# Weight chunks fetched behind 36 modulation pieces, and the first three output tiles multiplied feature by feature

## The chip, the cores and the metric

The kernel runs on one core of a Trainium2 chip. The core has TensorE (PE, matrix products into PSUM), VectorE (DVE), ScalarE (ACT), GpSimd (POOL, unused here) and SyncE (SP), which issues every transfer. All times are device microseconds (us) of the whole kernel; lower is better. Three runs of the kernel before gave 2514.09, 2517.24 and 2517.44 us.

## What is computed

Two transformer blocks on 256 tokens of width 1024, all in f32. Only the very start matters here: the condition vector gives shift, scale and gate by a large matrix-vector product, the input is normed and modulated, and the first SwiGLU follows.

```python
cond = silu(c)
mod = cond @ w_ada + b_ada                     # 1024 x 9216
sh1, sc1, gt1, ... = split(mod, 9)
u = rmsnorm(x, g1) * (1 + sc1) + sh1
a, b = split(u @ w_ffn1_in, 2)                 # 1024 x 5632
h = x + 0.5 * gt1 * ((silu(a) * b) @ w_ffn1_out)
...                                            # token mixing, FFN 2, block 2
```

## The kernel before

**Data.** X holds the tokens transposed, as 8 features groups ("features", k = 0 to 7) of 128 channels by 256 tokens. Every matrix is cut into chunks of 128 x 1024 numbers (512 KB); one chunk of a first FFN matrix makes one output tile of 128 channels, 8 products over k. Products are made in three matmuls each, since both factors are split into a rounded part ("high") and a remainder ("low"): high by high, high by low, low by high (L1404 to L1406). So one output tile is 24 matmuls of 256 columns.

**A weight chunk's way.** SyncE fetches it into one of four raw buffers (`fetch`, L1372). ScalarE rounds it into its own slot (`high`, L1652, own<-raw). VectorE subtracts that from the raw chunk (`low`, L1976), which frees the raw buffer; so fetch n waits for low n - 4. A slot is free when TensorE has done with the chunk that was in it (four slots at this stage).

**Modulation.** The nine sections of `w_ada` are 16 pieces of 128 x 512 each (256 KB, `modload`, L1362, into SCR or MODS). One pass of VectorE (`mod`, L1992) multiplies a piece by the condition vector and adds up; each pass is followed by a short accumulator read. The first 16 pieces give the scale sc1 (coefficient `CF`, L2013), the next 16 the shift sh1; both are needed before the first feature. 20 pieces can be on chip at the start; from piece 36 on, a piece's load waits for the pass of the piece four before it.

**The norm.** ScalarE squares the eight features (L1671), TensorE sums them over channels with a matrix of ones (L1431), ScalarE takes the root (`stat`, L1684) and VectorE the reciprocal (`root`, L2038). A feature is then a product on VectorE (`rms`, NT, L2112), a rounding on ScalarE (Uh, L1717) and a remainder on VectorE (Ul, L2119).

**Order.** Nothing is scheduled at run time. `schedule` calls methods of a `Plan`, each `put` appends one piece of work to a list, and every engine walks the list and takes what is its own, in that order. `chunk` is called when TensorE comes to a new chunk n: it puts the highs up to chunk n + 3 (`split_next`), then modulation passes by `rate` (`background`), and whatever was postponed. `low_parts` puts the lows of the highs so far, each followed by the next fetch; it does nothing for chunks above `low_limit`. `norm_tiles` puts the features; where it is given `tiles`, and nothing fills the time, it takes three chunks and puts `products` of all three after each feature. That way is in use later in the kernel, in the stages with other names than w1. In the first stage (`p.rms("n1", ...)`) the features are put alone, and the tiles come one after the other: chunk 0 is the "gate" half of output tile 0 (evicted by ScalarE with Silu, L1786, SA), chunk 1 its "up" half (multiplied in by VectorE, L2142, GT), then chunks 2 and 3 for tile 1. The product is split again (Hh on ScalarE, L1793, Hl on VectorE, L2148).

Of the kernel before, what the change touches and what calls it, by code (L numbers as in the profile page):

```python
# [25 lines left out]
SLABS = [[0, 1]] + [list(range(i, i + FS)) for i in range(2, FT, FS)]  # L26
# [4 lines left out]
LAT, CTX, BOTH = (0, S), (S, 2 * S), (0, 2 * S)  # L31
# [18 lines left out]
RING = 4  # L50
LEAD = 3
# [664 lines left out]
def schedule(total):  # L716
    p = Plan(total)
# [2 lines left out]
    while p.mod_fetch(0) and p.mod_loads < 16:  # L720
        pass
    p.put("xload")
    for _ in range(RING):
        p.fetch()
    p.put("cond", q=0, n=0)

    t = p.tally(LAT, False, lambda k: None)
    for k in range(KT):
        p.square(t, k, 0)
    p.rms("n1", 0, 0, "g1", (0, 0), None, ahead=LEAD)  # L730
    for who in (1, 2):
        p.put("condload", q=who, n=who)
        p.put("cond", q=who, n=who)
# [6 lines left out]
            p.put("rawshift", k=k, q=0, f=3)  # L740
        p.rate = 0.0

    main = p.ffn("w1", "w1o", LAT, [(("w1", 0), "half", 0, 2)], False, then={len(SLABS) - 1: before_raw}, raw="nm")
    p.put("ctxload")
    for _ in range(12):
        next(main)
    p.rate = 1.7
    p.put("maskload")
    for i in range(14):
        p.later(5 + i, lambda i=i: p.put("rotary", k=i))  # L750
# [22 lines left out]
    t = p.tallies.pop(LAT)  # L773
    raw = [p.raw_tile("wpqk", 0, 0, 6)]
# [15 lines left out]
    made, raw = raw, [None] * RAW  # L790
# [42 lines left out]
    n1 = 8  # L833
# [12 lines left out]
    for pair in range(4):  # L846
# [3 lines left out]
        c = p.chunk("wbr", pair)  # L850
# [24 lines left out]
    t = p.tallied(LAT, 1e-6, (0, 1))  # L875
# [156 lines left out]
    first = p.group("aqk", LAT, (*key_ctx["qs"], query))  # L1032
# [56 lines left out]
    t = p.tallies.pop(LAT)  # L1089
# [23 lines left out]
    t = p.tallied(LAT, 1e-5, (0, 0))  # L1113
# [1401 lines left out]
```

## Time and profile before

| | us |
|---|---|
| median of three runs | 2517.24 |
| profiled execution, own time | 2519.0 |
| its span | 2517.2 |
| TensorE busy | 2443.4 |
| first weight matmul | 42.93 |

The span is the time from the first to the last record of the trace; the own time of the same execution is 1.8 us longer. The granted clock of TensorE, as a mean over the span, is 0.991 of full speed. The 40 slices of the page show TensorE at 9 tenths in every slice from the second on; the first slice, 63 us long, has 4.

### The profile page before, as it was taken

What the parts mean: (1) busy time and instruction counts of PE and PEld (TensorE: products, weight loads), DVE (VectorE), ACT (ScalarE), POOL (GpSimd) and SP (SyncE); (2) the same over time, 40 slices, a digit from 0 to 9 for tenths busy, and PEclk for the clock granted to TensorE, in tenths of its full rate; (3) what the DMA queues carried; (4) which work ended last, traced back from release to release, by engine and by line L of the source; (5) the groups of instructions that cost most, each with busy time, mean ns of one, the idle gap of its engine ahead of it and who ended that gap; (6) DMA issues with size and microseconds to landing.
All of it is one profiled execution on the core that took longest, in us unless ns stands there. A gap on an engine that the chain in (4) does not pass through costs nothing.

```text
span 2517.2 us, 39580 instructions
## 1 busy us (share of the span) xinstructions
PE 2443.4 (97%) x15658; PEld 2223.6 (88%) x15658; DVE 1841.2 (73%) x3582; ACT 1138.0 (45%) x1754; POOL 0.2 (0%) x4
## 2 busy tenths in 40 slices
PE   4999999999999999999999999999999999999998
PEld 3999989999999888788888998888998888989997
DVE  7996977887779536768877669897776343677776
ACT  3445664544463324724223662232462222466664
POOL 0000000000000000000000000000000000000000
PEclk8999999999999999999999999999999999999999
DMA  8996656768867431654544256676365232222663
GB/s 315 345 346 204 214 173 237 252 232 292 294 204 243 137 101 59 211 157 126 154 136 125 88 181 198 197 235 195 123 226 167 93 126 92 73 93 91 195 194 100
DMA packets 161672, 454.73 MB, mean 181 GB/s; under 512 B 17744, under 2 KB 21328, under 8 KB 161488
## 3 DMA queue, kind: packets, MB, share of 16 engines
q1 hardware_dynamic: 161488, 452.21, 54.8%
q8 instruction: 124, 2.03, 0.3%
q14 instruction: 60, 0.49, 0.1%
HBM read 451.09 MB, written 1.05 MB: 180 GB/s over the span
## 4 chain that ended last, share of the span: by engine, by line
PE 75%; DVE 5%; ACT 4%; issue 1%; DMA 1%; SPq 0%; ACTq 0%; DVEq 0%
PE PS L1404 24%; PE PS L1406 23%; PE PS L1405 23%; DVE own L1976 1%; PE PS L1584 1%; PE PS L1431 1%; PE PS L1429 1%; ACT own L1652 1%; DMA MODS<-in_ma 1%; PE PS L1633 1%; DVE X L1957 1%; ACT Uh L1740 0%; PE PS L1616 0%; ACT NT L1744 0%; ACT X L1753 0%
## 5 line engine op out<-in xcount | busy, mean ns | idle before, releaser
L1652 ACT ACTIVATE own<-raw 128x1024 fp32r<-128x1024 f32 x425 | 444.2, 1053 | 344.2 <-PE PS L1406 247.3
L1404 PE MATMUL PS<-Uh,own 128*128 128x256 f32 (+1 forms) x1768 | 564.1, 319 | 24.3 <-DVE Ul L2119 17.2
L1976 DVE TENSOR_TENSOR own<-raw,own 128x1024 fp32r<-128x1024 f32 x425 | 515.6, 1219 | 71.4 <-ACT own L1652 71.0
L1405 PE MATMUL PS<-Ul,own 128*128 128x256 f32 (+1 forms) x1768 | 556.2, 315 | 0.0
L1406 PE MATMUL PS<-Uh,own 128*128 128x256 f32 (+1 forms) x1768 | 555.6, 314 | 0.0
L1404 PEld LDWEIGHTS PS<-Uh,own 128*128 128x128 f32 x1768 | 338.9, 192 | 49.4 <-issue 24.1
L1406 PEld LDWEIGHTS PS<-Uh,own 128*128 128x128 f32 x1768 | 339.0, 192 | 19.8
L1405 PEld LDWEIGHTS PS<-Ul,own 128*128 128x128 f32 x1768 | 339.0, 192 | 19.5 <-issue 0.2
L1404 PE MATMUL PS<-Hh,own 128*128 128x256 f32 (+1 forms) x1088 | 345.7, 318 | 1.1 <-DVE own L1976 0.6
L1405 PE MATMUL PS<-Hl,own 128*128 128x256 f32 (+1 forms) x1088 | 341.1, 314 | 0.0
L1406 PE MATMUL PS<-Hh,own 128*128 128x256 f32 (+1 forms) x1088 | 341.1, 313 | 0.0
L1957 DVE SCALAR_TENSOR_TENSOR X<-PS,CF,X 128x256 f32<-128x256 f32 x440 | 195.4, 477 | 109.0 <-PE PS L1406 108.8
L2142 DVE TENSOR_TENSOR GT<-SA,PS 128x256 f32<-128x256 f32 (+1 forms) x134 | 67.3, 502 | 279.8 <-PE PS L1406 277.2
L1404 PE MATMUL PS<-Uh,spare 128*128 128x256 f32 (+1 forms) x752 | 245.1, 326 | 0.6 <-DVE Ul L2135 0.6
L1405 PE MATMUL PS<-Ul,spare 128*128 128x256 f32 (+1 forms) x752 | 244.2, 325 | 0.0
L1406 PE MATMUL PS<-Uh,spare 128*128 128x256 f32 (+1 forms) x752 | 244.2, 325 | 0.0
L1404 PEld LDWEIGHTS PS<-Hh,own 128*128 128x128 f32 x1088 | 207.2, 190 | 15.1 <-DVE own L1976 0.8
L1405 PEld LDWEIGHTS PS<-Hl,own 128*128 128x128 f32 x1088 | 207.1, 190 | 12.4
L1406 PEld LDWEIGHTS PS<-Hh,own 128*128 128x128 f32 x1088 | 206.9, 190 | 12.2
L1652 ACT ACTIVATE spare<-raw 128x1024 fp32r<-128x1024 f32 x146 | 151.4, 1053 | 124.4 <-PE PS L1406 91.9
L1786 ACT ACTIVATE SA<-PS 128x256 f32<-128x256 f32 (+1 forms) x134 | 60.2, 449 | 306.8 <-PE PS L1406 306.6
L1976 DVE TENSOR_TENSOR spare<-raw,spare 128x1024 fp32r<-128x1024 f32 x146 | 176.4, 1217 | 9.1 <-ACT spare L1652 9.1
(263 smaller groups left out, 4404.6 us busy)
## 6 DMA issues: line engine op xcount, KB each, us to landing
MODS<-in_mm SPq DMA_DIRECT2D x168, 256.0 KB, 3.7
SCR<-in_mm SPq DMA_DIRECT2D x136, 256.0 KB, 4.1
raw<-in_f0i SPq DMA_DIRECT2D x68, 512.0 KB, 4.1
raw<-in_f1i SPq DMA_DIRECT2D x56, 512.0 KB, 3.5
raw<-in_f2i SPq DMA_DIRECT2D x56, 512.0 KB, 3.6
SCR<-in_ma SPq DMA_DIRECT2D x88, 256.0 KB, 5.4
raw<-in_w1i SPq DMA_DIRECT2D x44, 512.0 KB, 5.2
raw<-in_w2i SPq DMA_DIRECT2D x44, 512.0 KB, 4.8
```

Source lines behind the costliest of these rows:

```text
L1404: e.matmul(o, ll, rh, start=start, stop=False, skip_group_check=shared)
L1405: e.matmul(o, lh, rl, start=False, stop=False, skip_group_check=shared)
L1406: return e.matmul(o, lh, rh, start=False, stop=stop, skip_group_check=shared)
L1429: e.matmul(PS[:, w.bank[0], 0:S], ones[:, :], x, start=w.first, stop=w.final, skip_group_check=True)
L1431: e.matmul(PS[:, w.bank[0], S:2 * S], ones[:, :], sq, start=w.first and not w.centred, stop=w.final, skip_group_check=True).then_inc(s["ma ...
L1584: m = e.matmul(PS[:, w.bank[0], tt * P:(tt + 1) * P], VN[:, tt, w.f * P:(w.f + 1) * P], GW[:, g * P:(g + 1) * P], start=True, stop=True)
L1633: m = e.matmul(PS[:, w.bank[0], 0:P], v2[:, t, kv * P:(kv + 1) * P], PT2[:, w.k % 2, t * P:(t + 1) * P], start=(j == 0), stop=(j == 3))
L1652: e.activation(parts(w.n)[0], raw[:, w.n % RING, :], ACT.Copy).then_inc(s["whi"].tell(w.n), 1)
L1786: e.activation(SA[:, w.j % 2, lo:hi], PS[:, b, lo:hi], ACT.Silu).then_inc(s["gated"].tell(w.j), 1)
L1957: e.scalar_tensor_tensor(out=X[:, k, l:u], in0=part, scalar=cf((st, h))[:, k:k + 1], in1=X[:, k, l:u], op0=ALU.mult, op1=ALU.add).then_inc ...
L1976: e.tensor_tensor(low, raw[:, w.n % RING, :], high.bitcast(F32), ALU.subtract).then_inc(s["wlo"].tell(w.n), 1)
L2142: e.tensor_tensor(GT[:, w.j % 2, lo:hi], SA[:, w.j % 2, lo:hi], PS[:, b, lo:hi], ALU.mult).then_inc(s["product"].tell(w.j), 1)
```

## The change

The four fetches ahead of the modulation pieces are taken out. SyncE now issues all pieces up to the 36th before chunk 0; then chunks 0 to 6 as their waits allow. Four passes of the second 16 are put ahead of the three highs and the root. The lows of chunks 0 to 2 are held back by `low_limit` until all 32 passes are put. The features go through `norm_tiles` with tiles, so chunks 0, 1 and 2 are multiplied together, and `begin_ffn` puts the evictions of these three. The rate of passes is 1.8 after a while in place of 1.7.

```diff
     p.put("xload")
-    for _ in range(RING):
-        p.fetch()
     p.put("cond", q=0, n=0)
...
-    p.rms("n1", 0, 0, "g1", (0, 0), None, ahead=LEAD)
+    p.column(("n1", "c"), "g1", 0, 1)
+    for _ in range(4):
+        p.mod_step()
+    p.low_limit = -1
+    for _ in range(LEAD):
+        p.split_next()
+    t = p.tallied(LAT, 1e-6, (0, 0))
+    p.mod_until(0, 0)
+    p.low_limit = 1 << 30
+    first = p.norm_tiles("rms", "n1", t, LAT, (0, 0), None, p.ffn_tiles("w1"), q=0, f=0)
...
-    main = p.ffn("w1", "w1o", LAT, [(("w1", 0), "half", 0, 2)], False, then={len(SLABS) - 1: before_raw}, raw="nm")
+    p.begin_ffn("w1", first)
+    main = p.ffn("w1", "w1o", LAT, [(("w1", 0), "half", 0, 2)], False, early=1, then={len(SLABS) - 1: before_raw}, raw="nm")
     p.put("ctxload")
-    for _ in range(12):
+    for _ in range(10):
         next(main)
-    p.rate = 1.7
+    p.rate = 1.8
```

Line numbers of the changed kernel are 8 higher in the engines' code (L1652 becomes L1660). SyncE's transfers at the start, before (the row x3 holds chunks 4 to 6, in_ma the modulation pieces):

```order
L1362 DMA SCR<-in_ma 128x512 x16
L1364 DMA X<-in_xT 128x8x256
L1365 DMA ident<-in_ident 128x128
L1372 DMA raw<-in_w1i 128x1024 x4
L1362 DMA SCR<-in_ma 128x512 x16
L1362 DMA MODS<-in_ma 128x512
L1372 DMA raw<-in_w1i 128x1024 x3
```

and now:

```order
L1370 DMA SCR<-in_ma 128x512 x16
L1372 DMA X<-in_xT 128x8x256
L1373 DMA ident<-in_ident 128x128
L1370 DMA SCR<-in_ma 128x512 x16
L1370 DMA MODS<-in_ma 128x512 x2
L1370 DMA SCR<-in_ma 128x512 x2
L1380 DMA raw<-in_w1i 128x1024 x7
```

The four weight chunks stand behind 20 pieces that they were ahead of.

ScalarE from the squares to the first features, before (own<-raw are the highs, RS the root, Uh the features):

```order
L1671 ACTIVATE SQ<-X 128x256 x8
L1652 ACTIVATE own<-raw 128x1024 x3
L1684 ACTIVATE RS<-PS,small 128x256
L1717 ACTIVATE Uh<-NT,M 128x256 x8
L1655 ACT_TABLE_LOAD
```

and now:

```order
L1679 ACTIVATE SQ<-X 128x256 x8
L1660 ACTIVATE own<-raw 128x1024 x3
L1692 ACTIVATE RS<-PS,small 128x256
L1660 ACTIVATE own<-raw 128x1024
L1725 ACTIVATE Uh<-NT,M 128x256 x8
```

The order of highs and root is the same; a fourth high has come in behind the root.

VectorE behind the 16th pass, before (SCR,M is a pass, CF the scale, own the lows, NT and Ul the features, GT the product of an output tile):

```order
L2013 SCALAR_TENSOR_TENSOR CF<-M,V 128x8
L1976 TENSOR_TENSOR own<-raw,own 128x1024 x3
L2038 RECIPROCAL RS<-RS 128x256
L1992 ISA SCR,M<-SCR,V 128x512
...
L2112 SCALAR_TENSOR_TENSOR NT<-X,CF,RS 128x256 x2
...
L2142 TENSOR_TENSOR GT<-SA,PS 128x256
L1976 TENSOR_TENSOR own<-raw,own 128x1024
```

and now (four passes in the first place that is left out, twelve behind the reciprocal, the features before the low of chunk 3):

```order
L2021 SCALAR_TENSOR_TENSOR CF<-M,V 128x8
...
L2046 RECIPROCAL RS<-RS 128x256
L2000 ISA SCR,M<-SCR,V 128x512
...
L1984 TENSOR_TENSOR own<-raw,own 128x1024 x3
L2120 SCALAR_TENSOR_TENSOR NT<-X,CF,RS 128x256 x2
...
L1984 TENSOR_TENSOR own<-raw,own 128x1024
L2150 TENSOR_TENSOR GT<-SA,PS 128x256
L2000 ISA MODS,M<-MODS,SCR,V 128x512
L2000 ISA M 128x1
L2150 TENSOR_TENSOR GT<-SA,PS 128x256
L1984 TENSOR_TENSOR own<-raw,own 128x1024 x3
```

The three lows moved from ahead of the reciprocal to behind the last pass, and both products of the first two tiles stand ahead of the lows of chunks 4 to 6.

## Rows read from the trace of the kernel before

**Rows 1.** The page, part 1: busy us of each engine, share, instructions.

```profile
PE 2443.4 (97%) x15658; PEld 2223.6 (88%) x15658; DVE 1841.2 (73%) x3582; ACT 1138.0 (45%) x1754; POOL 0.2 (0%) x4
```

**Rows 2.** Waits of TensorE, whole span: engine, line, waited for, us, times, longest.

```profile
PE PS L1431 <- ACT SQ L1671: 21.1, 2, 20.3
PE PS L1404 <- DVE Ul L2119: 17.2, 4, 16.2
PE PS L1404 <- DVE own L1976: 5.8, 7, 1.7
```

**Rows 3.** Stretches: length, busy us (instructions) by engine; clock, DMA share, GB/s.

```profile
20.00:30.00 10.00, 6.43 (x16) 4.92 (x16) 4.51 (x4) 5.95 (x12) 0.00 (x0) 0.96 1.04 393
30.00:40.00 10.00, 0.00 (x0) 0.00 (x0) 10.00 (x30) 0.00 (x0) 0.00 (x0) 0.50 1.04 395
60.00:200.00 140.00, 140.00 (x1190) 139.97 (x1190) 127.84 (x265) 65.91 (x96) 0.00 (x0) 1.00 0.97 347
```

**Rows 4.** Timeline of SyncE's queue: start, us taken to issue.

```profile
9.63 0.65 SPq L1364 DMA_DIRECT2D X<-in_xT  x1
...
13.14 1.86 SPq L1372 DMA_DIRECT2D raw<-in_w1i  x4
15.04 11.34 SPq L1362 DMA_DIRECT2D SCR<-in_ma  x16
26.42 0.43 SPq L1362 DMA_DIRECT2D MODS<-in_ma  x1
26.90 2.85 SPq L1372 DMA_DIRECT2D raw<-in_w1i  x3
```

**Rows 5.** DMA issues, X and the 33rd piece: KB, us from issue to landing.

```profile
X<-in_xT SPq DMA_DIRECT2D x1, 1024.0 KB, 10.1
...
MODS<-in_ma SPq DMA_DIRECT2D x1, 256.0 KB, 11.1
```

**Rows 6.** Timeline of ScalarE, 19 to 28 us: start, us, work, idle before.

```profile
19.75 1.33 ACT L1671 ACTIVATE SQ<-X 128x256 f32<-128x256 f32 x4 [12.52 <-DMA X<-in_xT]
...
24.42 2.93 ACT L1652 ACTIVATE own<-raw 128x1024 fp32r<-128x1024 f32 x3
...
27.26 0.45 ACT L1684 ACTIVATE RS<-PS,small 128x256 f32<-128x256 f32 x1
```

**Rows 7.** Timeline of VectorE, 25 to 42 us.

```profile
25.49 3.49 DVE L1976 TENSOR_TENSOR own<-raw,own 128x1024 fp32r<-128x1024 f32 x3 [7.74 <-ACT own L1652]
...
28.90 1.75 DVE L2038 RECIPROCAL RS<-RS 128x256 f32<-128x256 f32 x1
...
30.57 0.65 DVE L1992 CUSTOM_DVE_ANT_0 SCR<-SCR,V 128x512 f32<-128x512 f32 x1
...
41.24 0.88 DVE L2112 SCALAR_TENSOR_TENSOR NT<-X,CF,RS 128x256 f32<-128x256 f32 x2
```

**Rows 8.** Timeline: first weight matmul; ScalarE behind the third and fourth tile.

```profile
42.93 0.55 PE L1404 MATMUL PS<-Uh,own 128*128 128x256 f32 x1 [16.18 <-DVE Ul L2119]
...
57.18 0.39 ACT L1786 ACTIVATE SA<-PS 128x256 f32<-128x256 f32 x1 [1.11 <-PE PS L1406]
...
60.07 1.06 ACT L1652 ACTIVATE own<-raw 128x1024 fp32r<-128x1024 f32 x1 [1.55 <-PE PS L1406]
```

**Rows 9.** Stretches around the first tiles, as rows 3; the clock is third from the end.

```profile
44.00:46.00 2.00, 2.00 (x8) 1.59 (x9) 1.93 (x6) 1.02 (x2) 0.00 (x0) 0.50 1.10 354
...
50.00:52.00 2.00, 2.00 (x12) 2.00 (x11) 0.00 (x0) 2.00 (x3) 0.00 (x0) 0.50 0.47 131
52.00:54.00 2.00, 2.00 (x14) 2.00 (x14) 1.28 (x2) 1.91 (x3) 0.00 (x0) 0.71 0.00 0
```

**Rows 10.** Timeline of VectorE: product of tile 0 and the low of chunk 4.

```profile
55.21 0.41 DVE L2142 TENSOR_TENSOR GT<-SA,PS 128x256 f32<-128x256 f32 x1
55.54 1.21 DVE L1976 TENSOR_TENSOR own<-raw,own 128x1024 fp32r<-128x1024 f32 x1
56.68 0.74 DVE L1992 CUSTOM_DVE_ANT_0 SCR<-SCR,V 128x512 f32<-128x512 f32 x1
```

**Rows 11.** Tight places: a piece's wait, chunk 17's low, chunk 19's high; landings 100 to 200.

```profile
94.23 0.75 DVE L1992 CUSTOM_DVE_ANT_0 MODS<-MODS,SCR,M 128x512 f32<-128x512 f32 x1 [4.37 <-DMA MODS<-in_ma]
...
94.90 1.22 DVE L1976 TENSOR_TENSOR own<-raw,own 128x1024 fp32r<-128x1024 f32 x1
...
96.15 1.06 ACT L1652 ACTIVATE own<-raw 128x1024 fp32r<-128x1024 f32 x1 [3.75 <-DMA raw<-in_w1i]
...
DMA to landing us min/median/max: 4.4/5.2/6.6
```

## Prediction, made before the changed kernel ran

> **What bounds the kernel now.** I read the busy times first. TensorE is busy 2443.4 us of a span of 2517.2 us, 97 % [rows 1], so almost everything that is not TensorE work lies in its idle time. The list of its waits comes next: two entries at the start make 36.5 us, 20.3 us before the sums of squares and 16.2 us before the first weight tile, and every other entry is 5.8 us or less [rows 2]. The reader should then look at the first tile's stage, the 140 us from 60 to 200: TensorE never idles there, 1190 matmuls, the memory engines busy 0.97 of the time at 347 GB/s and VectorE 127.8 us of 140 [rows 3]. So the path is: a head in which TensorE waits (to 42.9 us), then TensorE itself. A microsecond moved in the head arrives at the end, because no stretch behind it has slack that would take it back.
>
> The head in order of time. SyncE issues 16 modulation pieces, the input X, four weight chunks, and 16 further pieces [rows 4]. ScalarE has X at 19.75, squares it, then rounds three weight chunks ("highs", 24.42 to 27.3) and takes the root at 27.26 [rows 6]. VectorE makes the three remainders ("lows") from 25.49, the reciprocal at 28.90, 16 passes from 30.57 to 41.24, and then the eight features [rows 7]. The first weight matmul comes 1.69 us behind that, at 42.93; the third tile is finished at 57.18, when ScalarE takes it, and the fourth at 60.07 or just before [rows 8].
>
> **The weight transfers.** In the new order of SyncE all 36 pieces stand ahead of chunk 0. The three highs still stand ahead of the root on ScalarE, which runs in order. So chunk 2's arrival now sets the root. When is that? X landed at 9.63 + 10.1 = 19.7 us, and the 33rd piece at 26.42 + 11.1 = 37.5 us [rows 4, 5]. Between them lie 64 KB, four chunks of 512 KB and 17 pieces of 256 KB, 6.62 MB in 17.8 us, or 372 GB/s. Behind X there are now 64 KB, 20 pieces and three chunks, 6.88 MB, 18.5 us, so chunk 2 lands at 38.2 us. The ends are the window rates: 395 GB/s [rows 3] gives 37.1 us, the 347 GB/s of the later stage gives 39.5 us. I take 38.2, since it is from landings of the same stretch.
>
> The Trainium skill (DMA: Bandwidth & Descriptors, Specifications) states a limit of about 358 GB/s of memory for a core; by it chunk 2 would land at an estimated 38.9 us and the sum would be 0.7 us higher. The rows show 393 and 395 GB/s here, so the page's limit is passed while this core runs alone, and the row decides [rows 3].
>
> **The root.** The third high runs 38.2 to 39.2. The root's ACTIVATE takes 0.45, and the reciprocal takes 1.67 until the next pass may start (28.90 to 30.57) [rows 6, 7]: passes go on at 41.35. Before it was 30.57, so **+10.8 us**.
>
> **Four passes ahead.** One pass takes (41.24 - 30.57) / 16 = 0.667 us. Pieces 16 to 19 need 1.1 MB behind X, so they are in at 22.7 us, and the 7.74 us in which VectorE sat idle before 25.49 [rows 7] is the place where they run. They leave the path: 4 x 0.667 = **-2.7 us**. Twelve passes stay behind the reciprocal. Nothing hides them, since the features need the shift that they produce.
>
> **The lows.** Before, three of them ran from 25.49 to 28.90, beside ScalarE's work, and delayed the reciprocal by some 1.2 us (the root's value was there at 27.7). Now the three stand behind the twelve passes and ahead of the features: 28.90 - 25.49 = **+3.4 us**. Their old place costs nothing more to take away, since the reciprocal's start is already counted in the first term. The features then begin at 41.35 + 12 x 0.667 + 3.4 = 52.8 us in place of 41.24, which is +11.5, and the first matmul is at 54.4 us in place of 42.93.
>
> **Three tiles at once.** Before, a feature came every 0.9 us and gave TensorE three matmuls, 0.64 us at the low clock, and the second and third tile followed. Now each feature gives nine. At 1.2 GHz nine take 9 x 0.213 = 1.92 us, so TensorE is full from the first feature. The granted clock before was 0.5 to about 53.2 us (0.71 as a mean of 52 to 54) [rows 9]. TensorE was partly busy from 42.93 and without a gap only from 49.1. So the rise came 10.2 us after the first matmul and 4.1 us after the work became dense. I take 4.1 us, because the new work is dense from its first matmul; the other end is 10.2. 4.1 us hold 19 matmuls of 0.213; the other 53 run at 140 / 1190 = 0.118 [rows 3], 6.24 us; with 0.3 us until the result is seen, 10.6 us. Before, 42.93 to 57.18 were 14.25 us. So **-3.6 us**, and with the late rise it would be -0.8. VectorE isn't the limit: its eighth feature is out some 8 us after the first began.
>
> **A new wait behind the tiles.** In the new order of VectorE the product for output tile 1 (its "up" half is chunk 3) stands ahead of the lows of chunks 4, 5 and 6. Before, low 4 stood right behind the product of tile 0 [rows 10]. The product needs chunk 3's last matmul, 2.83 us after the third tile (60.0 against 57.18) [rows 8]. Then 0.33 for the product and 1.14 for the low: chunk 4 is ready 4.3 us after the third tile, where TensorE wants it at 2.6 (it issues ahead of the visible end). **+1.8 us**. Chunks 5 and 6 follow at 1.14 us each against TensorE's 2.83, so the queue is healed at once. ScalarE's two Silu passes over the condition vectors lie in its idle time before the third tile ends, and the highs 4 to 6 end ahead of the lows that want them.
>
> **What costs nothing.** The modulation rate of 1.8 in place of 1.7 makes up for five passes that are behind by chunk 3; the count is one behind at chunk 49. That is 0.1 x 0.667 us more per chunk on an engine with about 9 % free [rows 3]. If that cover were gone each chunk would cost 0.07 us, 3 us over 46 chunks; that is in the second rival below.
>
> **Sum**: 10.8 - 2.7 + 3.4 - 3.6 + 1.8 = +9.7 us on a span of 2517.2, so 2526.9. The profiled execution's own time is 2519.0 with 1.8 around the span; the median of the three runs is 2517.24, and added to that median the forecast is **2526.9 us**. With the transfer ends and the noise of the runs (2514.1 to 2517.4) its own range is 2523 to 2530.
>
> **Rival 1, not slower: the root isn't held.** If the weight copies got in ahead of the pieces, the root would be as early as TensorE's sums allow (27.7). Then reciprocal to 29.4, twelve passes to 37.4, three lows to 40.8: features 0.4 earlier, three tiles -3.6, the new wait +1.8, together -2.2, **2515.0 us**. For it: the trace of before shows no chunk queued behind 36 pieces, and four chunks had arrived in time. Against it: X and the 33rd piece arrived in the order and at the rate of the sum above. It decides by chunk 2's arrival: each microsecond after about 27 costs one, and the balance is nought at 29 us; 6.88 MB in the 9.3 us from X would be 740 GB/s against 393. The Trainium skill (DMA: Bandwidth & Descriptors, Queues, rings and completion order) says that data writes carry no barrier and a later one may finish before an earlier one, though each ring is consumed in order. That rule would allow small overtaking, and rows 5 show none that would matter.
>
> **Rival 2: a ring that is one chunk short.** Four chunks were fetched at the outset; now three, and each later fetch is issued with a low, one chunk (2.83 us) later than before, up to about chunk 141. A chunk must land, be rounded and have its low within three chunks, 8.5 us; landings took 4.4 to 6.6 us between 100 and 200 us [rows 11], and with 1.06 and 1.22 that is 6.7 to 8.9. ScalarE already waited 3.75 us for one chunk at 96 us, and VectorE 4.37 us for a piece, after which a low was ready only 0.7 us before TensorE's turn (96.05 against 57.2 + 14 x 2.83 = 96.8) [rows 11, 8]. With 0.13 us for each of some 12 tight chunks, 1 or 2 us at that wait, and 3 us if VectorE's cover goes, this adds up to 6: **2533 us**. Against it: 5.2 is the median, which fits.
>
> **Rival 3: the clock rises late.** If dense work doesn't bring it forward, -0.8 stands in place of -3.6: **2529.7 us**. For it: the clock stood at 0.5 all through the first tile's features [rows 9]. Against it: TensorE had gaps in each of those features, which the new order closes.
>
> **Chances.** Forecast 0.68, rival 1 0.10, rival 2 0.11, rival 3 0.10, anything faster by more 0.01. A measurement of this kernel tells about 0.2 %, 5 us, from no change. To be faster by that the head would have to gain 5.0 us, and the most that the sum allows with every loss gone is 2.2 to 4; 0.03. Within it: rival 1 and a thin tail of the forecast, 0.11. Slower: 0.86. The range reaches from 2522 to 2533.5: it leaves out rival 1, half of rival 2 and the forecast's lower tail.
>
> **What the new profile would show.** SyncE's chunk 0 issued around 23.5 us; ScalarE's first high at 35, its wait on the raw chunks some 10 us; the reciprocal at 39.7; VectorE idle for some 16 us before it, twelve passes behind it, first weight matmul at 54.4; the clock up by 58.5; the third tile done at 65.0; a wait of TensorE of 1.8 us for a low at 67.6; then 172 matmuls per 20 us as before. I am wrong if the reciprocal comes before 36 us, if TensorE waits in the stage from 75 to 230 us, or if a stretch behind 230 us is shorter than before by more than 1 us.

## The result, and the profile of the changed kernel

| | before | changed |
|---|---|---|
| median of 8 runs each, one chip, us | 2517.34 | 2523.54 |
| lowest to highest | 2513.61 to 2520.31 | 2521.56 to 2526.90 |
| profiled execution, own time / span | 2519.0 / 2517.2 | 2523.58 / 2521.8 |

The ratio is 1.0028, with an interval of 1.0019 to 1.0038: slower by 6.2 us. The sign and the range were right (2522 to 2533.5). The size, +9.7 us, was too large.

SyncE's queue in the changed kernel (start, us taken to issue), to be read against [rows 4]. Twenty pieces stand behind X, and only then come the chunks, with 24.45 in place of 13.14 as their start. The seven chunks are one group in this view: the first four issue at once, and the last three from 50.03 on, when their buffers are free. The condition vectors stand behind all seven.

```profile
13.58 8.45 SPq L1370 DMA_DIRECT2D SCR<-in_ma  x16
22.07 1.14 SPq L1370 DMA_DIRECT2D MODS<-in_ma  x2
23.25 1.15 SPq L1370 DMA_DIRECT2D SCR<-in_ma  x2
24.45 28.18 SPq L1380 DMA_DIRECT2D raw<-in_w1i  x7
52.67 0.91 SPq L1358 DMA_DIRECT2D SCR<-in_conds  x2
```

ScalarE, the rows that answer to [rows 6] and [rows 8] (in brackets the idle time before a row and its releaser). The first high waits 10.23 us for its chunk. The root (L1692) follows the third high at 38.64, where it was 27.26. The third tile is taken at 64.23, where it was 57.18.

```profile
35.14 1.06 ACT L1660 ACTIVATE own<-raw 128x1024 fp32r<-128x1024 f32 x1 [10.23 <-DMA raw<-in_w1i]
...
37.68 1.06 ACT L1660 ACTIVATE own<-raw 128x1024 fp32r<-128x1024 f32 x1 [0.20 <-DMA raw<-in_w1i]
38.64 0.46 ACT L1692 ACTIVATE RS<-PS,small 128x256 f32<-128x256 f32 x1
...
64.23 0.39 ACT L1794 ACTIVATE SA<-PS 128x256 f32<-128x256 f32 x1 [0.32 <-PE PS L1414]
```

VectorE, as [rows 7] and [rows 10]. It sits idle 15.32 us until the reciprocal, makes passes from 40.80 to 48.79, then the three lows, and the first feature at 52.20 in place of 41.24. The last row is the product behind chunk 3, which stands ahead of low 4.

```profile
39.13 1.75 DVE L2046 RECIPROCAL RS<-RS 128x256 f32<-128x256 f32 x1 [15.32 <-ACT RS L1692]
...
40.80 0.65 DVE L2000 CUSTOM_DVE_ANT_0 SCR<-SCR,V 128x512 f32<-128x512 f32 x1
...
48.79 3.49 DVE L1984 TENSOR_TENSOR own<-raw,own 128x1024 fp32r<-128x1024 f32 x3
...
52.20 0.87 DVE L2120 SCALAR_TENSOR_TENSOR NT<-X,CF,RS 128x256 f32<-128x256 f32 x2
...
67.07 0.42 DVE L2150 TENSOR_TENSOR GT<-SA,PS 128x256 f32<-128x256 f32 x1 [1.96 <-PE PS L1414]
```

TensorE's first weight matmul, for [rows 8]:

```profile
53.88 0.55 PE L1412 MATMUL PS<-Uh,own 128*128 128x256 f32 x1 [26.55 <-DVE Ul L2127]
```

TensorE's waits over the whole span, for [rows 2] (us in total, times, longest). The wait for features is longer by 10.3 us. The entry for lows is 6.2 us against 5.8, and 1.6 of it is a new wait at chunk 4.

```profile
PE PS L1412 <- DVE Ul L2127: 27.5, 4, 26.5
...
PE PS L1412 <- DVE own L1984: 6.2, 7, 1.7
```

Stretches of the changed kernel, with the columns of [rows 3]. The clock, third from the end, is 0.58 and then 1.00. TensorE is dense from its first matmul, has a gap only behind chunk 3 (2.35 us busy of 4 from 66 to 70), and then runs 172 to 173 matmuls in 20 us with no gap.

```profile
54.00:58.00 4.00, 4.00 (x21) 4.00 (x22) 3.86 (x10) 2.08 (x5) 0.00 (x0) 0.58 1.01 356
58.00:62.00 4.00, 4.00 (x36) 4.00 (x35) 2.83 (x5) 3.56 (x5) 0.00 (x0) 1.00 1.00 357
66.00:70.00 4.00, 2.35 (x20) 2.15 (x20) 2.93 (x4) 2.41 (x4) 0.00 (x0) 1.00 0.71 214
80.00:100.00 20.00, 20.00 (x173) 20.00 (x172) 18.55 (x39) 9.01 (x12) 0.00 (x0) 1.00 1.00 357
180.00:200.00 20.00, 20.00 (x173) 20.00 (x172) 20.00 (x44) 9.95 (x20) 0.00 (x0) 1.00 1.00 366
```

The wait behind chunk 3 is 1.65 us in the timeline, from 67.03 to 68.68.

So the head is as predicted, but the end isn't as late as the head. To see where the difference goes, I matched TensorE's matmuls, of which every trace has the same 15658 in the same order, between the trace of before and each other trace. The table gives how much later, in us, each kernel starts the matmul that before starts at the time in the head of the column. The experiments are in it already.

| kernel | ring behind the start | 68 | 210 | 333 | 347 | 400 | 475 | 1400 | end |
|---|---|---|---|---|---|---|---|---|---|
| changed | 3 | +9.0 | +8.9 | +8.9 | +8.6 | +8.6 | +6.6 | +6.6 | +4.6 |
| e1 root first | 3 | -3.6 | -3.7 | -3.7 | -4.2 | -4.1 | -6.8 | -6.7 | -7.9 |
| e2 fetch only | 3 | +8.6 | +8.4 | +8.4 | +7.8 | +7.8 | +5.6 | +5.6 | +4.4 |
| e4 low 4 first | 3 | +8.7 | +9.0 | +9.0 | +8.2 | +8.2 | +6.4 | +6.4 | +4.1 |
| e5 rate 1.7 | 3 | +10.3 | +10.2 | +10.2 | +10.0 | +10.0 | +10.4 | +10.4 | +10.2 |
| e8 e1, e4, fetches earlier | 3 | -5.4 | -5.5 | -5.5 | -4.9 | -4.9 | -7.0 | -7.0 | -8.1 |
| e9 chunk 3 too | 3 | -6.8 | -6.1 | -6.1 | -5.3 | -5.4 | -7.5 | -7.4 | -8.6 |
| e11 no passes | 3 | +8.7 | +8.6 | +8.7 | +10.2 | +10.2 | +7.7 | +9.0 | +6.6 |
| e3 tiles only | 4 | +4.6 | +4.5 | +4.5 | +0.8 | +0.8 | +1.9 | +1.9 | +0.8 |
| e6 before, rate 1.8 | 4 | -1.4 | +1.8 | +2.3 | -1.4 | -1.4 | -1.7 | -1.7 | -3.2 |
| e7 ring of four | 4 | +15.3 | +16.3 | +16.3 | +14.4 | +14.4 | +14.7 | +14.7 | +14.3 |
| e10 tiles, vectors first | 4 | -0.8 | -0.9 | -0.9 | -3.1 | -3.1 | -3.0 | -2.9 | -3.9 |

Three things in the first row weren't in the prediction: what happens between 333 and 347 us (a later section takes it apart), the 2.0 us that come back between 400 and 475, and the 2.0 us that come back behind 1400.

**The part behind 1400 us is the clock's.** In the trace of before the clock is at its lower level until 53.2 us, from 336.5 for 6.8 us, from 1462.9 for 3.4 and from 1841.8 for 3.4. In the trace of the changed kernel it is so until 57.4 and from 347.5 for 3.4 us, and then not before the last 7 us. Each of the two later dips takes 1.4 or 1.5 us off the changed kernel's lateness while it lasts; waits behind it give 0.5 back, so that some 1.0 is left. Two stretches of before (clock 0.61 and 0.60):

```profile
1462.00:1466.00 4.00, 4.00 (x24) 4.00 (x24) 3.20 (x4) 2.91 (x6) 0.00 (x0) 0.61 0.48 155
1842.00:1846.00 4.00, 4.00 (x24) 4.00 (x23) 3.12 (x4) 2.72 (x5) 0.00 (x0) 0.60 0.49 144
```

The same work in the changed kernel, at 1.00:

```profile
1466.00:1470.00 4.00, 1.99 (x17) 2.02 (x17) 3.49 (x7) 3.04 (x6) 0.00 (x0) 1.00 0.72 236
1846.00:1850.00 4.00, 3.04 (x25) 3.07 (x26) 3.12 (x7) 4.00 (x7) 0.00 (x0) 1.00 0.42 142
```

Which dips occur differs from profile to profile: of the 13 profiles here, ten have the one near 1460 and three the one near 1842 (before, e5 and e7). The profiled execution of before lies 1.7 us above the median of its runs, and that of the changed kernel on its median. So of the gap between the profiled difference of 4.6 us and the medians' +6.2 the choice of executions makes 1.6, and the medians are the better figure.

### The profile page after: what moved, and what is told of

It reads as the page before. It is cut to its first block, busy times and chain, and to the rows that moved or that the text cites. A ratio compares the mean times of both kernels' runs of the same rounds, so it can differ in the third digit from the quotient of the medians.

```text
span 2521.8 us, 39579 instructions
## 1 busy us (share of the span) xinstructions
PE 2435.1 (97%) x15658; PEld 2216.7 (88%) x15658; DVE 1840.6 (73%) x3582; ACT 1138.7 (45%) x1754; POOL 0.2 (0%) x4
## 4 chain that ended last, share of the span: by engine, by line
PE 75%; DVE 6%; ACT 4%; issue 1%; DMA 0%; ACTq 0%; DVEq 0%; SPq 0%
PE PS L1412 23%; PE PS L1413 23%; PE PS L1414 23%; DVE own L1984 1%; ACT own L1660 1%; PE PS L1592 1%; PE PS L1439 1%; PE PS L1437 1%; ACT Uh L1748 1%; ACT NT L1752 1%; PE PS L1641 1%; DVE X L1965 1%; PE PS L1624 0%; ACT spare L1660 0%; DVE X L2138 0%
## 5 line engine op out<-in xcount | busy, mean ns | idle before, releaser
L1660 ACT ACTIVATE own<-raw 128x1024 fp32r<-128x1024 f32 x425 | 444.5, 1054 | 382.0 <-PE PS L1414 235.2
L2150 DVE TENSOR_TENSOR GT<-SA,PS 128x256 f32<-128x256 f32 (+1 forms) x134 | 67.4, 503 | 281.3 <-PE PS L1414 275.9
L1412 PEld LDWEIGHTS PS<-Hh,own 128*128 128x128 f32 x1088 | 206.8, 190 | 14.4 <-DVE own L1984 0.8
L1660 ACT ACTIVATE spare<-raw 128x1024 fp32r<-128x1024 f32 x146 | 151.4, 1053 | 127.8 <-PE PS L1414 91.9
```

What stands on the lines that cost most here:

```text
L1412: e.matmul(o, ll, rh, start=start, stop=False, skip_group_check=shared)
L1660: e.activation(parts(w.n)[0], raw[:, w.n % RING, :], ACT.Copy).then_inc(s["whi"].tell(w.n), 1)
L2150: e.tensor_tensor(GT[:, w.j % 2, lo:hi], SA[:, w.j % 2, lo:hi], PS[:, b, lo:hi], ALU.mult).then_inc(s["product"].tell(w.j), 1)
```

## The experiments

Each ratio is against runs of before that were made beside the experiment. Their medians are 2518.2 us for e1 to e4, 2516.4 for e5 to e8 and 2517.1 for e9 to e11, so medians from different groups compare to 1 or 2 us only.

**e1: the root ahead of the highs.** The claim to test: the root's place behind three highs that wait for weights is what costs. Same transfers, same passes, one line moved.

```diff
+    t = p.tallied(LAT, 1e-6, (0, 0))
     for _ in range(LEAD):
         p.split_next()
-    t = p.tallied(LAT, 1e-6, (0, 0))
```

> The changed kernel with one edit: on ScalarE the root of the norm stands ahead of the first three highs. My theory (the root was held by chunk 2's landing, which cost 10.8 us of the head): the reciprocal starts at about 27.8 us in place of 39.13, twelve passes end at about 37.5, the three lows then wait for nothing but the last high (over at 38.7) and end at about 40.9; first weight matmul at about 42.5 in place of 53.9, so 11.4 us off the changed kernel: about 2512 us. Rival (the head is long because the transfers of 36 pieces and the chunks behind them are slow, whatever waits for them): the first weight matmul stays later than 50 us and the time within 2 us of the changed kernel's 2523.5.

Measured 2512.31 us, ratio 0.9981 (0.9972 to 0.9991). VectorE of e1:

```profile
26.27 1.75 DVE L2046 RECIPROCAL RS<-RS 128x256 f32<-128x256 f32 x1 [3.65 <-ACT RS L1692]
...
35.92 3.72 DVE L1984 TENSOR_TENSOR own<-raw,own 128x1024 fp32r<-128x1024 f32 x3
39.57 0.87 DVE L2120 SCALAR_TENSOR_TENSOR NT<-X,CF,RS 128x256 f32<-128x256 f32 x2
```

The reciprocal comes 12.9 us sooner than in the changed kernel and the first feature 12.6 us sooner. The passes now run while the chunks arrive, and the whole loss is gone: by the medians 11.2 us are gained against the changed kernel, and 5.9 against before (the ratio's interval is 2 to 7 us). So late weights need not cost what they cost here; e8 and e9 below show that they aren't free either. It was the order of one in-order queue, ScalarE's, that turned them into a loss.

**e2: the late fetch alone.** Before, with the four early fetches left out. Nothing else of the change; the ring behind the start is then three deep as well.

```diff
     p.put("xload")
-    for _ in range(RING):
-        p.fetch()
```

> The kernel before with the four early fetches taken out and nothing else: tiles one after the other, all 16 passes behind the reciprocal, lows ahead of it. Chunk 0 stands behind 33 pieces. My theory: chunk 2 lands at about 36.1 us, its low ends at about 38.3, reciprocal 38.3 to 40.0, sixteen passes to 50.6, first weight matmul at about 52.3 (9.4 later than in the kernel before) and the third tile 9.4 later: 2517.3 + 9.4 = 2526.7 us. Rival (the late fetch costs little by itself, the loss came with the order of passes and tiles): within 3 us of 2517.

Measured 2523.69 us, 1.0029 (1.0018 to 1.0040).

```profile
34.41 3.76 DVE L1974 TENSOR_TENSOR own<-raw,own 128x1024 fp32r<-128x1024 f32 x3 [16.14 <-ACT own L1650]
38.09 1.74 DVE L2036 RECIPROCAL RS<-RS 128x256 f32<-128x256 f32 x1
...
50.43 0.87 DVE L2110 SCALAR_TENSOR_TENSOR NT<-X,CF,RS 128x256 f32<-128x256 f32 x2
```

The first feature is 9.2 us later than before, as forecast (+9.4), and the time is that of the whole change. The fetch is the change's cost; the rest of it nets about nothing. The end is 3 us better than expected; 2.2 of them are the give-back between 400 and 475 us.

**e3: the three tiles alone.** Before with its early fetches, and only the features spread over three tiles.

```diff
-    p.rms("n1", 0, 0, "g1", (0, 0), None, ahead=LEAD)
+    first = p.rms("n1", 0, 0, "g1", (0, 0), None, ahead=LEAD, tiles=p.ffn_tiles("w1"))
...
-    main = p.ffn("w1", "w1o", LAT, [(("w1", 0), "half", 0, 2)], False, then={len(SLABS) - 1: before_raw}, raw="nm")
+    p.begin_ffn("w1", first)
+    main = p.ffn("w1", "w1o", LAT, [(("w1", 0), "half", 0, 2)], False, early=1, then={len(SLABS) - 1: before_raw}, raw="nm")
```

> The kernel before with the fetches as they were and only the first three output tiles multiplied feature by feature. My theory: first weight matmul at 42.9 us as before; the clock rises some 3.4 to 5 us after it instead of 10.2; third tile done at about 53.2 to 54 in place of 57.18, a new wait of TensorE of 1.6 us for the low of chunk 4; net about 2.4 us earlier at the fourth tile, and 2515 us. Rival (the clock rises at the same 53 us as in the kernel before whatever TensorE does): third tile at about 56.5, with the new wait 1 us later than before, 2518 us.

Measured 2519.76 us, 1.0012 (1.0003 to 1.0021): a miss by 4.8 us. Stretches of e3, the clock third from the end:

```profile
46.00:50.00 4.00, 4.00 (x32) 4.00 (x32) 3.75 (x8) 2.81 (x4) 0.00 (x0) 0.88 0.00 0
58.00:62.00 4.00, 0.25 (x1) 0.25 (x2) 2.87 (x6) 4.00 (x6) 0.00 (x0) 0.83 0.35 113
62.00:66.00 4.00, 4.00 (x20) 4.00 (x21) 4.00 (x8) 1.70 (x4) 0.00 (x0) 0.50 0.81 238
```

TensorE's wait for lows in e3, from 42 to 80 us:

```profile
PE PS L1405 <- DVE own L1977: 5.4, 1, 5.4
```

ScalarE's two Silu passes in e3, with the waits before them in brackets:

```profile
54.99 1.06 ACT L1656 ACTIVATE SCR<-SCR 128x1024 f32<-128x1024 f32 x1 [5.20 <-DMA SCR<-in_conds]
...
57.70 1.06 ACT L1656 ACTIVATE SCR<-SCR 128x1024 f32<-128x1024 f32 x1 [1.65 <-DMA SCR<-in_conds]
```

And SyncE's queue in e3, chunk 7's fetch and what stood behind it:

```profile
50.17 0.33 SPq L1373 DMA_DIRECT2D raw<-in_w1i  x1
50.54 0.91 SPq L1351 DMA_DIRECT2D SCR<-in_conds  x2
```

The tiles themselves gained: the clock was up at 47.0 (first row), where it was 53.2 before, and at 57 us TensorE was 3.6 us ahead of before. But ScalarE's two Silu passes over the condition vectors waited 5.20 and 1.65 us. SyncE had issued the vectors only at 50.54, directly behind chunk 7's fetch, which waits in the queue until low 3 has freed its buffer. Behind the Silu passes on ScalarE stood the third tile's eviction and the highs of chunks 4 to 6, so TensorE waited 5.4 us, and the clock was low again from 60.6 to 67.4. Before, the vectors were issued at 32.20, ahead of chunk 7's fetch at 53.98, and this didn't arise. In the changed kernel the vectors stand behind the seventh chunk and not the eighth, and both Silu passes ran at 60.70 without waiting for them.

**e10: e3 with the condition vectors ahead.** Their two loads stand ahead of the root and the features.

```diff
+    for who in (1, 2):
+        p.put("condload", q=who, n=who)
     first = p.rms("n1", 0, 0, "g1", (0, 0), None, ahead=LEAD, tiles=p.ffn_tiles("w1"))
     for who in (1, 2):
-        p.put("condload", q=who, n=who)
         p.put("cond", q=who, n=who)
```

> The kernel before with three tiles feature by feature, and the two further condition vectors loaded right behind chunks 0 to 3, so that ScalarE's Silu passes don't wait for them as they did with the tiles alone (6.9 us). Theory: the wait of 5.4 us behind chunk 3 falls to 1.6, the clock doesn't fall again at 60 us, first weight matmul at about 42.9, the fourth tile done at about 57.5 in place of 60.0, and 2515 us. Rival (three tiles at once gain nothing by themselves, since VectorE's and ScalarE's work behind them is bunched): 2517 us or more.

Measured 2515.27 us, 0.9992 (0.9983 to 1.0001), 4.5 us under e3. The wait of 5.4 us is now 1.6 us, as in the changed kernel, and the clock doesn't fall there. At 68 us this kernel is 0.8 ahead of before, where the prediction's terms -3.6 and +1.8 give -1.8. The clock rose at 49.0 us here and at 47.0 in e3: 2.0 us more at half speed, which would account for the missing 1.0.

**e11: the four passes left out.** The passes ahead of the sums were a term of -2.7 us.

```diff
     p.column(("n1", "c"), "g1", 0, 1)
-    for _ in range(4):
-        p.mod_step()
     p.low_limit = -1
```

> The changed kernel without the four passes ahead of the root: all sixteen stand behind the reciprocal. Theory: four passes of 0.67 us come on to the path, reciprocal still at 39.1, first weight matmul at about 56.6 in place of 53.9, 2526 us. Rival (the passes are hidden behind the transfers either way): 2523.5 us.

Measured 2524.38 us, 1.0026 (1.0017 to 1.0036): the changed kernel's time, within the intervals. VectorE of e11:

```profile
36.51 1.75 DVE L2044 RECIPROCAL RS<-RS 128x256 f32<-128x256 f32 x1 [19.06 <-ACT RS L1690]
...
52.26 0.89 DVE L2118 SCALAR_TENSOR_TENSOR NT<-X,CF,RS 128x256 f32<-128x256 f32 x2
```

SyncE's queue in e11 around the first chunks:

```profile
21.39 0.55 SPq L1368 DMA_DIRECT2D MODS<-in_ma  x1
21.98 1.75 SPq L1378 DMA_DIRECT2D raw<-in_w1i  x3
23.77 0.43 SPq L1368 DMA_DIRECT2D MODS<-in_ma  x1
```

I had held the reciprocal to stay at 39.1; it came at 36.51. Every step of the passes also issues a load when a buffer comes free. Without the four steps 17 pieces stand behind X and ahead of chunk 0, and with them 20. The three pieces are 0.79 MB, an estimated 2.1 us by the prediction's 372 GB/s. From X's landing to chunk 2's the traces have 17.55 us (20.11 to 37.66) in the changed kernel and 15.55 (19.49 to 35.04) here, so the three loads cost 2.0 us. The other 0.6 is that X itself landed earlier in this profile, with the same work ahead of it. The features begin at 52.26 and 52.20. So the four passes save 2.7 us and their loads cost 2.0, as long as the root hangs on chunk 2; the 0.7 that this leaves is less than the medians can tell.

**e4: low 4 ahead of the product.** The changed kernel, with chunk 4's low moved ahead of tile 1's product on VectorE.

```diff
         n = self.chunk(name, i, lead)
+        if n == 3:
+            self.low_parts(1)
         w = self.put(what, st=st, n=n, r=r, bank=self.bank(), **fields)
```

> The changed kernel with one edit: on VectorE the low of chunk 4 stands ahead of the product of output tile 1. My theory: TensorE's wait of 1.6 us between chunk 3 and chunk 4 is gone, everything behind it is 1.6 us earlier: about 2522 us. Rival (the low would have been late anyway, since its high is not ready earlier): the wait stays over 1 us and the time 2523.5.

Measured 2523.16 us, 1.0024 (1.0014 to 1.0034). The stretches of e4:

```profile
58.00:62.00 4.00, 4.00 (x27) 4.00 (x26) 3.20 (x6) 3.23 (x4) 0.00 (x0) 0.71 1.03 377
66.00:70.00 4.00, 4.00 (x35) 3.95 (x34) 3.26 (x5) 3.28 (x5) 0.00 (x0) 1.00 0.59 184
```

The wait is gone: 35 matmuls from 66 to 70 us against 20. In this profile the clock rose at 60.3, 2.9 us later than in the changed kernel (0.71 in the first row, against 1.00), and at 68 us the gain is 0.3. The median is 0.4 us lower, which a measurement doesn't resolve. That the wait was caused by the order of the product and low 4 is shown; that removing it gains 1.6 us at the end isn't.

**e7: a fourth chunk in the ring again.** One fetch behind the three highs.

```diff
     for _ in range(LEAD):
         p.split_next()
+    p.fetch()
```

> The changed kernel with one more fetch put behind the first three, so that each later fetch again stands four lows behind. Two things are expected. At the start the fetch of chunk 7, which waits for low 3 (over at about 61 us), now stands ahead of the two condition vectors on SyncE; they land at about 65.5 and 67, ScalarE's Silu passes hold the evictions of the first tiles, and TensorE waits some 5 us for the low of chunk 4 in place of 1.6. Under theory H the 2 us between 430 and 480 are lost as well: about 2529 us. Under the rival that the shorter ring is itself a loss in the long stage (rival 2 of the prediction) the stage from 80 to 230 us would be shorter than in the changed kernel.

Measured 2531.52 us, 1.0062 (1.0047 to 1.0077). Chunk 7's fetch again stands ahead of the condition vectors, as in e3; TensorE waits 3.6 us for a low, and the clock is low again from 71.1 to 77.9. The time is 2.5 us above the expected 2529. From 68 to 210 us this kernel loses another 1.0 us where the changed kernel loses none, so a fourth chunk gains nothing in the long stage.

**e5 and e6: the modulation rate.** The changed kernel with the rate 1.7, and before with 1.8.

```diff
-    p.rate = 1.8
+    p.rate = 1.7
```

> The changed kernel with the modulation rate left at 1.7. What is asked: in the trace the changed kernel is 8.6 us behind at 430 us and only 6.6 at 480, because TensorE no longer waits for lows in the gate stage. Theory H (the ring that is one chunk shorter): VectorE's waits for modulation pieces there (2.1 us before, 0.4 after) went because weight fetches now stand one chunk later in SyncE's queue; then the rate is beside the point, the 2 us are still given back, and the time is 2523.5 within 1 us. Rival R (the rate of 1.8 shifted the passes against the lows): the 2 us aren't given back, 2525.5 us.

> The kernel before with the rate 1.8 in place of 1.7 and nothing else (four chunks fetched at the outset). Theory H: TensorE's waits for lows between 440 and 475 us stay at about 1.9 us, the time is that of the kernel before within 1 us, 2517 to 2518. Rival R: the waits go, some 2 us faster, 2515.5.

e5: 2523.89 us, 1.0036 (1.0023 to 1.0049). e6: 2517.71, 1.0007 (0.9997 to 1.0017). Neither differs from its partner by more than a measurement can tell, so the rate is not where the time went. In e6 TensorE loses 3.2 us between 68 and 210, where it waits three times for lows, and has it back by 347; its profile has no dip of the clock near 336, and that is 3.1 of it. Its waits for lows at 456 and 472 us stay, so the rate alone doesn't take them away. The profile of e5 is its slowest run (2529.23) and has one dip more than others, at 469.8.

**e8 and e9: what the experiments point to.** e8 is e1 with nine passes ahead of the sums in place of four, the three fetches ahead of them, and e4's line. e9 fetches chunk 3 at the outset too and leaves out one later fetch, so that behind the start its ring holds three, as in the changed kernel.

```diff
-    for _ in range(4):
+    for _ in range(LEAD):
+        p.fetch()
+    for _ in range(9):
         p.mod_step()
     p.low_limit = -1
+    t = p.tallied(LAT, 1e-6, (0, 0))
     for _ in range(LEAD):
         p.split_next()
-    t = p.tallied(LAT, 1e-6, (0, 0))
```

> The root ahead of the highs, chunks 0 to 2 fetched ahead of pieces 34 to 36, nine passes instead of four ahead of the root, and the low of chunk 4 ahead of the product of tile 1. Theory: each holds a different place of the head. Chunk 2's high ends at about 36.6 us, the passes at about 34.2, the lows at 37.7, first weight matmul at about 39.4 (42.5 expected with the root moved alone), and 1.6 us less behind chunk 3: four to five microseconds below the 2512.3 us of the kernel with the root moved alone, so about 2508. Rival (the pieces' landing bounds the head once the root is free): first weight matmul at 42 us or later and 2511 us.

> The kernel with the four edits, and chunk 3 fetched ahead of the last pieces as well (the next fetch is left out once, so that the ring is as deep as in the changed kernel). There the fourth high waited 2.26 us for chunk 3 and held the first feature's rounding behind it. Theory: it lands at about 36.7 us, the first rounding is no longer held, first weight matmul at about 39.3 us in place of 40.7, and 1.4 us less at the end: about 2509.5 us. Rival: the pieces of the second section that now land later, or the lows, hold the features instead, and nothing is gained (2511).

e8: 2510.95 us, 0.9979 (0.9970 to 0.9988), the rival's time and not the theory's. Its first weight matmul came at 40.94 and not at 39.4. e9: 2509.74 us, 0.9968 (0.9956 to 0.9981), its first weight matmul at 39.19. ScalarE of e8, the fourth high and the features' high half behind it:

```profile
38.82 1.06 ACT L1664 ACTIVATE own<-raw 128x1024 fp32r<-128x1024 f32 x1 [2.26 <-DMA raw<-in_w1i]
39.79 0.89 ACT L1729 ACTIVATE Uh<-NT,M 128x256 fp32r<-128x256 f32 x2
```

The same two in e9:

```profile
36.56 1.06 ACT L1669 ACTIVATE own<-raw 128x1024 fp32r<-128x1024 f32 x1 [0.23 <-DMA raw<-in_w1i]
38.02 0.91 ACT L1734 ACTIVATE Uh<-NT,M 128x256 fp32r<-128x256 f32 x2 [0.41 <-DVE NT L2129]
```

In e8 the fourth high waited 2.26 us for chunk 3, and the features' high half (Uh) stood behind it on ScalarE: the fault of the change once more, one chunk further on. e9 takes it away, and Uh comes 1.8 us sooner. e1, e8 and e9 all beat both kernels; e9 is the fastest by median, by 7.4 us against before's 2517.1 in the same comparison. The intervals of e9 and e1 overlap, so that it is better than e1 isn't settled.

## Why the prediction was right in sign and too large

**The weight transfers, right to 0.5 us.** Chunk 2's high began at 37.68; the forecast for its landing was 38.2. The 6.88 MB behind X took 17.55 us, 392 GB/s: the window rate, which the prediction had as its lower end, and not the 372 of its middle. These 0.5 us are most of what the head's steps were off. The Trainium skill's limit for a core (DMA: Bandwidth & Descriptors, Specifications), which the page derives as half of what two cores share, would have had it land at an estimated 38.9; with one core at work the row was the better guide.

**The root, right.** Forecast +10.8; the passes go on at 40.80 in place of 30.57, which is +10.2. e1 shows the mechanism by undoing it.

**Four passes ahead, -2.7: a true term whose price I had put in another term.** The 20 pieces ahead of chunk 2 were in the sum of the transfers, but I didn't see that three of them were there only because of the passes. As working for the whole change it was right, as a statement of what the passes are worth it was wrong: by e11 they gain 0.7 us at most.

**The lows, +3.4, right.** 48.79 to 52.20 is 3.41. With the two terms above the first feature is 11.0 later (forecast 11.5) and the first matmul came at 53.88 (54.4).

**Three tiles, forecast -3.6, measured -3.9** (+10.95 at the first matmul, +7.05 at the third tile). The clock rose 3.5 us after the first matmul here (4.1 assumed), so rival 3 didn't come about in this trace. It isn't a fixed number, though: it rose 6.1 to 6.2 us after it in e4, e5 and e7, where TensorE's work up to there is the same. That the term came out so near was in part luck.

**The new wait, right.** 1.65 us from 67.0 against 1.8 at 67.6, at the place and with the cause named; e4 shows the cause. From chunk 4 on TensorE stood at +9.0 us. The sum up to there was +9.7, so the head's steps were wrong by 0.7 us together.

**"What costs nothing" held here, for a reason that wasn't mine.** The Silu passes lay in idle time because the condition vectors weren't behind a fetch that waits. Where the tiles are together and the ring has four chunks they were, and at 68 us that had cost 5.4 us (e3 against e10) and 6.3 (e7 against the changed kernel), with the clock's part in it. I had looked at ScalarE's time and not at SyncE's queue.

**The step that failed: "no stretch behind it has slack that would take it back".** Between 400 and 475 us 2.0 us come back; a stretch behind 230 us that is shorter by more than 1 us was one of the prediction's own signs of being wrong. [rows 2] had shown 5.8 us of waits for lows, and this is where 1.9 of them lay. TensorE waits there for lows, and VectorE for pieces. In before, from 432 to 500 us:

```profile
PE PS L1404 <- DVE own L1976: 1.9, 2, 1.3
DVE MODS L1992 <- DMA MODS<-in_ma: 1.7, 3, 1.1
```

In the changed kernel, in the same work, from 441 to 509 us:

```profile
PE PS L1412 <- DVE own L1984: 0.6, 1, 0.6
DVE SCR L2000 <- DMA SCR<-in_ma: 0.4, 1, 0.4
```

The table shows across kernels with what this goes. All kernels with three chunks in the ring, except e5, gain 1.8 to 2.7 us between 400 and 475, whatever their head. All with four stay within 1.1 us, e7 among them, which is the changed kernel with one fetch more. e5 moves by +0.4: TensorE waits 2.0 us for a low there, up to 468.9, and the clock's dip at 469.8 comes behind that wait. A reading that fits: with one chunk less queued the pieces land sooner, VectorE waits less for them, and its lows come in time. That the gain goes with the ring's depth is shown in these pairs, with e5 as the one exception. That it acts by this path is argued from the waits, and why e5 lacks it stays open.

**Rival 2 had the right cause, and the wrong place and size.** From 75 to 230 us, where I expected the short ring to cost up to 6 us, TensorE had no wait at all, and its shift stays at +8.9 up to 333. A price falls due at 336 us, where TensorE waits for VectorE's X. ScalarE waits for chunks before that, VectorE's lows stand behind ScalarE, and X behind the lows. In before, from 300 to 330 us, and TensorE's wait in the stretch to 337:

```profile
ACT own L1652 <- DMA raw<-in_f0i: 0.7, 1, 0.7
PE PS L1537 <- DVE X L1957: 2.0, 1, 2.0
```

In the changed kernel, from 308 to 339 us, and to 347:

```profile
ACT own L1660 <- DMA raw<-in_f0i: 3.4, 3, 2.0
PE PS L1545 <- DVE X L1965: 3.4, 1, 3.4
```

This wait is 2.7 to 3.6 us in the kernels with three chunks, except e5 (1.8), and 1.4 to 2.1 in those with four. In the changed kernel it takes the shift from +8.9 to +10.2. At 347 us it is +8.6, because the low clock behind the wait lasted 3.4 us here and 6.8 in before, which is worth 1.6. Where that dip is as long as in before (e8, e9, e11) the price can still be seen at 347: 0.6 to 1.5 us. So the short ring's price at 336 is 1.3 us and its gain behind 400 is 2.0, and the sum of the two was small, as the forecast had it for another reason.

**The sum, closed.** In the profiles: +9.0 at chunk 4, -0.1 to 333, +1.3 for the wait at 336, -1.6 for the clock there, -2.0 between 400 and 475, and -2.0 for the clock's dips near 1463 and 1842: +4.6. Without the clock's three parts it is +8.2. The forecast of +9.7 was thus too large by 0.7 in the head and by 0.8 behind it; that leaves 2.0 us to the medians' +6.2. They are as large as two dips of the clock, and no trace shows which dips the other runs had. The lowest runs of the two kernels (2513.61 and 2521.56) lie 8.0 apart, which fits that before's usual run loses some 2 us more to dips; it isn't shown.

## What to carry to other kernels

When a load is put later in a queue, look for the first instruction of each in-order engine that waits for it, and at what stands behind that instruction: here a root of 0.46 us cost 10 us, because three copies that weren't urgent stood ahead of it. A step that "only moves work into idle time" also issues its loads; count them ahead of whatever the path waits for (here three pieces took back 2.0 of the 2.7 us that four passes saved). And a prefetch ring is not free at its deep end: a fetch that waits for its buffer holds every later transfer of that queue, so its depth is to be tried both ways: one chunk less cost 1.3 us in one stage here and gave 2.0 us in another.

## What the hardware showed that I had not expected

- The clock's rise behind the first dense matmul wasn't a constant. With nearly the same work it came 3.5 us after it in the changed kernel (53.88 to 57.4), and 6.1 us in e4 (54.26 to 60.3). Over the ten kernels that multiply three tiles at once it was 2.8 (e11) to 6.2 us (e5). The difference between the first two costs about 1.2 us and is as large as a term of the sum.
- Once up, it was low again for 6.8 us (60.6 to 67.4) in e3, where TensorE was idle for 5.4 us up to 61.8, and for 6.8 us (71.1 to 77.9) in e7 around an idle time of 3.6 us, so that such a wait costs more than itself: while it is low a matmul takes 0.21 us in place of 0.12.
- Dips of 3.4 or 6.8 us at the same places of the program came in some profiles and not in others (336 to 354 us: 6.8 in before, e5, e8, e9 and e11, none in e3 and e6, 3.4 in the rest). Here they moved the end by 1.0 to 1.6 us for 3.4 us, and by 3.1 for 6.8. Each of them except one (e11, near 716) began within 2 us behind an idle time of TensorE of 1.5 to 3.6 us; but the idle time of 2.0 us near 1460 is in every trace and has no dip behind it in three. Between the two main profiles they make 3.6 us, which is more than half of what was measured.
